# Differential attention taken two heads at a time, with the dense matmul job beside it cut in four parts

## The reference, cut to what matters

```python
def diff_attention(q, k, v, lam):            # q (B,Lq,H,2,dh), k (B,Lk,H,2,dh), v (B,Lk,H,2dh)
    s = jnp.einsum('bqhcd,bkhcd->bhcqk', qi, k).astype(jnp.float32) * scale
    p = jax.nn.softmax(s, axis=-1)
    pd = (p[:, :, 0] - lam * p[:, :, 1]).astype(v.dtype)
    return jnp.einsum('bhqk,bkhe->bqhe', pd, v)
```

## Time and profile before

| what | value |
|---|---|
| median of 3 runs | 1815.11 us (1813.92, 1815.11, 1817.08) |
| profiled execution, first to last instruction (span) | 1814.2 us |
| its TensorE busy / VectorE busy / ScalarE busy | 1664.4 / 510.3 / 299.0 us |
| its mean granted TensorE clock, as a share of 2.4 GHz | 0.982 |
| its HBM traffic | 634.14 MB read, 3.70 MB written |
| attention loop in it | 273.8 to 388.5 us |

### The profile page before, as it was taken

How to read it: one execution, slowest core, us unless ns; L and a number is a source line. 1 busy time by engine, 2 the same in 40 slices (tenths; PEclk the granted TensorE clock), 3 DMA queues, 4 the chain that set the end, 5 groups by cost and what they waited for, 6 DMA issues and landing times.

```text
span 1814.2 us, 19110 instructions
## 1 busy us (share of the span) xinstructions
PE 1664.4 (92%) x7868; PEld 781.6 (43%) x7868; DVE 510.3 (28%) x982; ACT 299.0 (16%) x636; POOL 47.9 (3%) x72
## 2 busy tenths in 40 slices
PE   6999999999999999999888988989888889989897
PEld 3767787778873333333222322323223233323332
DVE  4575647775770201111010111101011111101103
ACT  2553354463320000000000000000000000000001
POOL 2010000011000000000000000000000000000001
PEclk9999999999989999999999999999999999999999
DMA  9782232226598999999999999999999999999996
GB/s 352 270 293 96 81 128 93 93 89 198 219 388 333 426 427 431 429 432 428 429 432 430 431 430 432 428 432 429 430 430 431 431 429 431 430 429 430 429 430 269
DMA packets 65310, 638.51 MB, mean 352 GB/s; under 512 B 5685, under 2 KB 5869, under 8 KB 36589
## 3 DMA queue, kind: packets, MB, share of 16 engines
q1 hardware_dynamic: 61936, 629.83, 83.3%
q0 software_dynamic: 3328, 8.04, 1.6%
HBM read 634.14 MB, written 3.70 MB: 352 GB/s over the span
## 4 chain that ended last, share of the span: by engine, by line
DMA 49%; PE 47%; DVE 3%; issue 0%; ACT 0%; SPq 0%; ACTq 0%; DVEq 0%
DMA ring<-in_w_exp_gate 23%; DMA ring<-in_w_exp_up 23%; PE banks L887 17%; PE banks L1290 15%; DMA ring<-in_w_exp_down 3%; PE banks L1407 3%; PE banks L885 2%; PE banks L839 1%; PE banks L1272 1%; PE banks L902 1%; PE banks L1088 1%; PE banks L883 1%; PE banks L1045 1%; PE banks L1019 1%; PE banks L1109 1%; DMA ring<-in_w_mod 1%
## 5 line engine op out<-in xcount | busy, mean ns | idle before, releaser
L1290 PE MATMUL banks<-ring,O 128*64 128x512 f32 x3048 | 656.6, 582 | 79.5 <-DMA ring<-in_w_exp_up 59.7
L1290 PEld LDWEIGHTS banks<-ring,O 128*64 128x64 f32 x3048 | 211.1, 135 | 527.5 <-issue 423.9
L1407 PE MATMUL banks<-ring,O 128*64 128x512 f32 x1400 | 320.6, 613 | 35.1 <-DMA ring<-in_w_exp_down 30.7
L1407 PEld LDWEIGHTS banks<-ring,O 128*64 128x64 f32 x1400 | 99.8, 141 | 244.9 <-issue 187.5
L887 PE MATMUL banks<-slot_parts,X_parts 128*128 128x512 f32 x672 | 184.3, 403 | 0.0
L2234 DVE TENSOR_TENSOR O<-O,banks 128x512 f32<-128x512 f32 (+1 forms) x48 | 30.9, 643 | 514.8 <-PE banks L1290 486.4
L1718 ACT ACTIVATE O<-banks 128x512 f32<-128x512 f32 (+1 forms) x48 | 23.7, 562 | 724.2 <-PE banks L1290 724.2
L887 PEld LDWEIGHTS banks<-slot_parts,X_parts 128*128 128x128 f32 x672 | 121.2, 188 | 39.4 <-issue 11.0
L2214 DVE TENSOR_TENSOR X<-X,banks 128x512 f32<-128x512 f32 x90 | 61.9, 688 | 188.1 <-PE banks L1272 188.1
L2247 DVE TENSOR_TENSOR O<-banks,O 128x512 f32<-128x512 f32 x32 | 20.7, 686 | 319.8 <-PE banks L1407 319.8
L1844 DVE TENSOR_TENSOR slot_parts<-ring,slot_parts 128x512 fp32r<-128x512 f32 x168 | 105.7, 688 | 15.3 <-ACT slot_parts L1463 14.6
(11 more groups left out here) (294 smaller groups left out, 1109.1 us busy)
## 6 DMA issues: line engine op xcount, KB each, us to landing
ring<-in_w_exp_up SPq DMA_DIRECT2D x61, 2816.0 KB, 33.8
ring<-in_w_exp_gate SPq DMA_DIRECT2D x58, 2816.0 KB, 32.1
ring<-in_w_exp_down SPq DMA_DIRECT2D x28, 3072.0 KB, 28.2
ring<-in_w_exp_down SPq DMA_DIRECT2D x13, 4096.0 KB, 31.6
ring<-in_w_in SPq DMA_DIRECT2D x16, 2048.0 KB, 9.0
ring<-in_w_exp_down SPq DMA_DIRECT2D x25, 1024.0 KB, 32.9
ring<-in_w_exp_down SPq DMA_DIRECT2D x7, 2048.0 KB, 12.5
ring<-in_w_mod SPq DMA_DIRECT2D x16, 512.0 KB, 11.4
```

What stands on the lines that cost most here:

```text
L1290: x = pe.matmul(banks[64 * w:64 * w + 64, 3 * m + b, 0:(i1 - i0) * P], xeT[:, 2 * (k % 4) + k // 4, :], w4[:, w, i0 * P:i1 * P], start=(k ...
L1407: x = pe.matmul(banks[64 * w:64 * w + 64, (4 if last else 6) + dc, :], hidT[:, i, 64 * w:64 * w + 64], rows[:, w, dc * BANK:(dc + 1) * BAN ...
```

## The change

TensorE's loop takes two items per round. A round has the scores of i and i+1, then a whole job in four parts of two tiles (six matmuls each), with the turning of i-2 after the first part, the turning of i-1 after the second, the output of i-2 after the third and the output of i-1 after the fourth. ScalarE's round has the four exponentials of the pair, then the two copies of turned probabilities, then the two output copies and squares; the job's copy stands at the end. The `silu` of row tiles 1 and 2 moves behind the loop. VectorE takes both maxima and one scaling for the pair, two tiles of the split, both differences with one reciprocal, two more tiles, and the job's copy.

```diff
--- before.py
+++ after.py
@@ -1113,20 +1113,23 @@
             for j in J_VD[-2:]:
                 wait_job_copied(pe, j)
             n = len(ATT_ITEMS)
-            for i in range(n + 2):
+            for i in range(0, n + 2, 2):
                 if i < n:
                     att_scores(i)
-                if i < n:
-                    job(ATT_JOBS[i // 2], KT // 2 * (i % 2), KT // 2 * (i % 2 + 1))
-                if i == n:
-                    job(J_GB[0], 0, 2)
-                if 1 <= i <= n:
+                    att_scores(i + 1)
+                j = ATT_JOBS[i // 2] if i < n else J_GB[0]
+                job(j, 0, 2)
+                if i:
+                    att_turn(i - 2)
+                job(j, 2, 4)
+                if i:
                     att_turn(i - 1)
-                if i > n:
-                    job(J_GB[0], 2, 6)
-                if i >= 2:
+                job(j, 4, 6)
+                if i:
                     att_out(i - 2)
-            job(J_GB[0], 6, KT)
+                job(j, 6, KT)
+                if i:
+                    att_out(i - 1)
             job(J_GB[1])
             pe.wait_ge(oa_g, T)
             for k in range(KT):
@@ -1599,28 +1602,38 @@
 
                 act.activation(ra[:, t, :], ra[:, t, :], ACT.Silu).then_inc(gates_on, 1)
 
+            def probs_copied(i):
+
+                nk = 1 if ATT_ITEMS[i][0] == 0 else 3
+                act.wait_ge(att_t, i + 1)
+                cp(pp[i % 2][3][:, 0:nk * P], banks[:, 6, 0:nk * P]).then_inc(att_tcp, 1)
+
+            def out_copied(i):
+
+                t, h = ATT_ITEMS[i]
+                act.wait_ge(att_o, i + 1)
+                b = banks[:, 7, 0:P]
+                link(cp(o_d[:, t, h * P:(h + 1) * P], b))
+                act.activation(b, b, ACT.Square, accum_out=s("eb", i, i + 1)).then_inc(att_ocp, 1)
+
             n = len(ATT_ITEMS)
-            for i in range(n + 2):
+            for i in range(0, n + 2, 2):
                 if i < n:
                     exps(i)
-                if i == n:
+                    exps(i + 1)
+                else:
                     for j in (J_RA[-1], J_RA[-2]):
                         wait_job_copied(act, j)
                     gla_gate(0)
-                if 1 <= i <= n:
-                    nk = 1 if ATT_ITEMS[i - 1][0] == 0 else 3
-                    act.wait_ge(att_t, i)
-                    cp(pp[(i - 1) % 2][3][:, 0:nk * P], banks[:, 6, 0:nk * P]).then_inc(att_tcp, 1)
-                if i >= 2:
-                    t, h = ATT_ITEMS[i - 2]
-                    act.wait_ge(att_o, i - 1)
-                    b = banks[:, 7, 0:P]
-                    link(cp(o_d[:, t, h * P:(h + 1) * P], b))
-                    act.activation(b, b, ACT.Square, accum_out=s("eb", i - 2, i - 1)).then_inc(att_ocp, 1)
-                if i >= n:
-                    gla_gate(i - n + 1)
-                if i < n and i % 2 and JOBS[ATT_JOBS[i // 2]].engine == "a":
+                if i:
+                    probs_copied(i - 2)
+                    probs_copied(i - 1)
+                    out_copied(i - 2)
+                    out_copied(i - 1)
+                if i < n and JOBS[ATT_JOBS[i // 2]].engine == "a":
                     job_copy(ATT_JOBS[i // 2])
+            for t in range(1, T):
+                gla_gate(t)
 
             act.wait_ge(att_ocp, n)
             act.activation(s("eb", 24, 48), s("eb", 0, 24), ACT.Sqrt, scale=1.0 / (2 * DH), bias=s("eps")).then_inc(od_sq, 1)
@@ -1995,40 +2008,42 @@
             family_copies(dve, F_KT, lambda h, b: dve.tensor_copy(kT[:, h, :], b), 1, lambda k: split(10, k - 1, k + 1))
 
             def neg_max(i):
-                t, h = ATT_ITEMS[i]
-                nk = SEQ if t == 0 else NKEY - SEQ
-                m = 2 * (i % 2)
-                dve.wait_ge(att_s, i + 1)
-                link(dve.tensor_reduce(s("mx", m, m + 2), banks[:, 2 + m:4 + m, 0:nk], AX.X, ALU.max))
-                if i >= 2:
-                    dve.wait_ge(att_e, 2 * (i - 1))
-                dve.tensor_scalar(s("nb", m, m + 2), s("mx", m, m + 2), -DH ** -0.5, None, ALU.mult).then_inc(att_nb, 1)
-
-            def difference(i):
-
-                t, h = ATT_ITEMS[i]
-                nk = SEQ if t == 0 else NKEY - SEQ
-                m = 2 * (i % 2)
-                p0, p1, pd, _ = (x[:, 0:nk] for x in pp[i % 2])
-                dve.wait_ge(att_e, 2 * (i + 1))
-                link(dve.reciprocal(s("rs", m, m + 2), s("sum", m, m + 2)))
-                note(dve.tensor_scalar(p1, p1, s("rs", m + 1, m + 2), s("nlam"), ALU.mult, ALU.mult))
+
+                nk = SEQ if ATT_ITEMS[i][0] == 0 else NKEY - SEQ
+                for m in range(2):
+                    dve.wait_ge(att_s, i + m + 1)
+                    note(dve.tensor_reduce(s("mx", 2 * m, 2 * m + 2), banks[:, 2 + 2 * m:4 + 2 * m, 0:nk], AX.X, ALU.max))
                 settle()
-                if i >= 2:
-                    dve.wait_ge(att_t, i - 1)
-                dve.scalar_tensor_tensor(out=pd, in0=p0, scalar=s("rs", m, m + 1), in1=p1, op0=ALU.mult,
-                                         op1=ALU.add).then_inc(att_pd, 1)
-
-            n = len(ATT_ITEMS)
-            for i in range(n + 2):
-                if i < n:
-                    neg_max(i)
-                if 1 <= i <= n:
-                    difference(i - 1)
-                if i < n and i % 2 and JOBS[ATT_JOBS[i // 2]].engine == "v":
+                if i:
+                    dve.wait_ge(att_e, 2 * i)
+                dve.tensor_scalar(s("nb"), s("mx"), -DH ** -0.5, None, ALU.mult).then_inc(att_nb, 2)
+
+            def differences(i):
+
+                nk = SEQ if ATT_ITEMS[i][0] == 0 else NKEY - SEQ
+                dve.wait_ge(att_e, 2 * (i + 2))
+                link(dve.reciprocal(s("rs"), s("sum")))
+                for m in range(2):
+                    p1 = pp[m][1][:, 0:nk]
+                    note(dve.tensor_scalar(p1, p1, s("rs", 2 * m + 1, 2 * m + 2), s("nlam"), ALU.mult, ALU.mult))
+                settle()
+                if i:
+                    dve.wait_ge(att_t, i)
+                for m in range(2):
+                    p0, p1, pd, _ = (x[:, 0:nk] for x in pp[m])
+                    dve.scalar_tensor_tensor(out=pd, in0=p0, scalar=s("rs", 2 * m, 2 * m + 1), in1=p1, op0=ALU.mult,
+                                             op1=ALU.add).then_inc(att_pd, 1)
+
+            for i in range(0, len(ATT_ITEMS), 2):
+                n, p = divmod(i // 2, 3)
+                neg_max(i)
+                if p:
+                    split(11 + n, 4 * p - 4, 4 * p - 2)
+                differences(i)
+                if p:
+                    split(11 + n, 4 * p - 2, 4 * p)
+                if JOBS[ATT_JOBS[i // 2]].engine == "v":
                     job_copy(ATT_JOBS[i // 2])
-                if i < n and i % 6 >= 2:
-                    split(11 + i // 6, 2 * (i % 6) - 4, 2 * (i % 6) - 2)
 
             dve.wait_ge(oa_n, T)
             for t in range(T):
```

## The result

The changed kernel takes 1821.22 us (median of 6 runs, 1820.75 to 1822.57) against 1815.66 us (6 runs of the kernel before, 1813.92 to 1817.59). The ratio is 1.0031, 95% interval 1.0021 to 1.0041: 5.6 us slower, where 7.8 us slower was forecast. Its profiled execution has a span of 1820.2 us and took 1822.04 us.

A forecast was written before the change was run, and what follows sets the result against it. TensorE's own list was taken to set the loop's pace. Context -1.4, latent +6.3, last round +0.8 and behind the loop +2.1 summed to +7.8 us, from 1815.1 to 1822.9; range 1817.5 to 1827.

The forecast's parts named there:

- ScalarE's copy gates the round: Latent pairs: the copy freeing bank 6 stands behind four exponentials, so TensorE waits 1.07 us; rounds 10.59 against 9.60.
- TensorE's own work: Latent pair: TensorE's own list takes 9.46 us against 9.60, the cuts costing about what the single switch saves.
- the rival without the gate: Attention loop: the copy doesn't gate and TensorE stays the bound; -4.2 us, or -2.1 with the later wait; chance 0.10.
- the wait behind the loop: Turnings of `o_a`: two `silu` now follow the last output, so the third turning waits for ScalarE's copy; +2.1 us.
- Context pairs: First eight items: no wait for the copy, an old wait gone and one switch saved in four pairs; -1.4 us.
- The latent part: Eight latent pairs: +0.99 us each from the wait for ScalarE's copy, less the three old waits; +6.3 us.
- The last round and the turnings behind it: Last loop round, TensorE waits 1.1 us for ScalarE: +0.8 us; then `o_a` turnings, behind two `silu`: +2.1 us.
- The DMA, VectorE and the stages that follow: Chunk loads released later still land in time, VectorE doesn't bind, loop time counts one for one at the end; no cost.
- The rival in which it falls: Attention loop: the granted clock falls after eight waits of 1.1 us; 1828 us; chance 0.08.

The follow-up runs named there:

- other_bank: Changed kernel, with the turning of an odd item sent to the job bank not in use; 1811.4 us, ratio 0.9975 to the kernel before.
- longer_chain: Changed kernel, with one more 384-column ScalarE copy behind the four exponentials in eight latent rounds; 1826.71 us, ratio 1.0066 to the kernel before.
- scaling_per_item: Changed kernel, with the first item's maximum scaled before the second is taken; 1815.2 us, ratio 0.9998 to the kernel before.
- copy_between_exps: Changed kernel, with ScalarE copying the turned i-2 between the exponentials of i and i+1; 1815.43 us, ratio 0.9998 to the kernel before.
- silu_between: Changed kernel, with the `silu` of row tile 1 between the last two output copies; 1821.53 us, ratio 1.0039 to the kernel before.

## Why the prediction was right

The direction, the mechanism and its place were as forecast. By its own steps:

- **ScalarE's copy gates the round.** Forecast: 5.97 us from the first score to the second turning, a wait of 1.07, rounds of 10.59. Measured: 5.97, 1.10 and 10.53. Shown by taking the gate away (other_bank), lengthening the chain (longer_chain) and shortening it at VectorE's end (scaling_per_item). Copy_between_exps confirms that the order is what matters, though its gain was smaller than expected. That the wait came out as forecast is in part luck: TensorE reached the second turning at 4.70, not 4.90, so the real wait was 1.27, and the records show 0.17 less of it.
- **TensorE's own work.** I forecast 9.46 a pair; it is 9.24 (other_bank). I had taken the fused scores at 1.70, the upper end of 1.4 to 1.70, and they cost 1.49 (342.49 - 341.00). It made no difference to the latent rounds of the changed kernel, as I had said, for there the chain decides. It does explain other_bank: the rival without the gate, with the wait behind the loop kept, was priced at -2.1 us, and the 0.21 in each of eight rounds and the 0.9 of the next point bring that to -4.7; the median was 4.8 under the kernel before.
- **Context pairs.** This term was mis-sized: -1.4 forecast (its two parts, 0.6 and four times 0.18, add to 1.3), -2.3 measured. There TensorE is the bound, so the price of the fused scores does count. A group of eight context score matmuls takes 0.65 us, where I had 0.84, in each of four rounds (0.8 us together).
- **The latent part.** +6.3 forecast, +5.8 measured: eight rounds, each 0.06 shorter than I had it (10.53 against 10.59).
- **The last round and the turnings behind it.** +0.8 and +2.1 forecast, +0.8 and +2.0 measured, and silu_between shows the second one's cause. Here the loss splits between the first dense part and the third turning.
- **The DMA, VectorE and the stages that follow.** Costed at nothing, and TensorE waited for none of them in the loop. VectorE's quarter of spare time was real but thin: once the rounds are shorter (other_bank, copy_between_exps), its splits hold up the maxima of some rounds.
- **The clock.** The rival in which it falls didn't come: it was granted 1.00 through eight waits of 1.1 us. I had also misread what came ahead of the low clock in the router stage of the kernel before. The granted clock fell while TensorE was still busy without a break, and its waits of over a microsecond (1.25 us to 530.37 and 1.74 us to 539.11) came after that:

```profile
526.00:528.60 2.60, 2.60 (x24) 2.55 (x23) 2.53 (x5) 0.00 (x0) 0.00 (x0) 1.00 1.03 428
528.70:529.10 0.40, 0.40 (x3) 0.31 (x2) 0.37 (x2) 0.00 (x0) 0.00 (x0) 0.50 1.50 625
```

  So nothing in that stage spoke for a fall after such waits; why the clock fell there stays open.

The sum was +7.8 against +6.3 measured between the same two places, and +5.6 in the medians. 1.4 of the 1.5 us between the first two are the context and the latent term; the 0.7 between the trace and the medians is less than single executions agree to.

## What to carry to other kernels

When work is taken in pairs, every buffer that is released once per item is a new gate: the second item waits until the first has been copied, and that copy may now stand behind the whole pair's work on its engine. Before grouping, follow each single buffer's release through the list of the engine that gives it, and count from the start of the round; a chain longer than the bound engine's way to the same place is paid in every round, however idle the engines look. The remedy was cheap here: a second buffer (10.4 us), or one small instruction issued per item (some 6 us).

## What the runs showed of the hardware that I hadn't expected

Scores of two heads one after the other run faster than two separate groups: eight matmuls in 1.49 us where two groups of four took 0.85 each, and in the context items 0.65 against twice 0.42. The weight loads of all eight were made while matmuls were in flight: in the row below, of the changed kernel's timeline, they take 0.95 us of the 1.56 us of their matmuls, although these alternate between the same two halves of the rows.

```profile
340.99 0.95 PEld L1088 LDWEIGHTS banks<-ring 64*128 64x128 f32 x8
```

The rule of the Trainium skill on this ("TensorE: Matmul & The Clock Gate", Part 3: an overlap only where the row groups differ) had been weighed against a row of before; by it I had counted some 0.05 us more for a fused group than for two single ones. The trace disagrees again: the fused group is 0.21 us shorter.
